# Taking the sixteen gate tiles out of the attention's filling, in a decoder layer on one core

## What is computed

```python
h = rms_norm(x, g_pre_mix)
cb, cc, ch, q, k, v, ga, gb = jnp.split(h @ w_in, IN_SPLITS, axis=-1)
conv_u, conv_state = causal_dwconv(cc * ch, conv_prev, w_conv_a)
y_a = (cb * conv_u) @ w_a
...
z = jnp.einsum('bqhd,bkhd->bhqk', q, k) * (SB_HEAD_DIM ** -0.5) + bias
a = exp(log_beta + later)         # a product of kept shares over later keys
o = jnp.einsum('bhqk,bkhd->bqhd', a, v)
y_b = o @ w_b
merged = jax.nn.sigmoid(ga) * y_a + jax.nn.sigmoid(gb) * y_b
x = x + rms_norm(merged @ w_o, g_post_mix)
```

## Time and profile before

| | before |
|---|---|
| median of 3 runs | 1683.26 us (1683.05 to 1683.74) |
| the profiled execution | 1683.39 us, of which its span is 1681.6 us |
| PE busy, PEld busy | 1668.7 us (99%), 1463.4 us (87%) |
| DVE busy | 1102.6 us (66%) |
| ACT busy | 794.6 us (47%) |
| granted TensorE clock | 1.00 in all slices but the end |

### The profile page before, as it was taken

One profiled execution on the slowest core, in us unless ns is written; L12 is line 12 of the kernel. 1 busy time (PEld: TensorE's weight loads), 2 busy tenths in 40 slices (PEclk: granted clock), 3 DMA queues, 4 the chain that ended last, 5 costly groups with the idle time before them and its releaser, 6 DMA issues. The chain is left out here.

```text
span 1681.6 us, 27183 instructions
## 1 busy us (share of the span) xinstructions
PE 1668.7 (99%) x9107; PEld 1463.4 (87%) x9107; DVE 1102.6 (66%) x1608; ACT 794.6 (47%) x1389; POOL 317.9 (19%) x266
## 2 busy tenths in 40 slices
PE   9999999999999999999999999999999999999998
PEld 8999998999999989988888888888888788888886
DVE  7265246325533647547678888888888698776576
ACT  6445344444534453135444444444444444465675
POOL 1000000000000000003356666666664000000000
PEclk9999999999999999999999999999999999999999
DMA  5312221132123114443132222222222852345333
GB/s 177 102 55 74 78 78 56 57 99 68 61 66 94 51 62 149 155 164 121 62 97 79 79 78 76 73 73 79 79 79 90 300 192 78 94 146 188 108 125 119
DMA packets 176599, 170.66 MB, mean 101 GB/s; under 512 B 16207, under 2 KB 144555, under 8 KB 176492
## 3 DMA queue, kind: packets, MB, share of 16 engines
q1 hardware_dynamic: 165546, 164.41, 30.3%
q10 hardware_dynamic: 10946, 4.91, 1.0%
HBM read 129.66 MB, written 39.62 MB: 101 GB/s over the span
## 5 line engine op out<-in xcount | busy, mean ns | idle before, releaser
L2810 PE MATMUL pair<-xh,wh 128*128 128x384 f32 (+1 forms) x952 | 324.3, 341 | 0.0
L2812 PE MATMUL pair<-xh,wl 128*128 128x384 f32 (+1 forms) x952 | 311.2, 327 | 0.0
L2811 PE MATMUL pair<-xl,wh 128*128 128x384 f32 (+1 forms) x952 | 310.6, 326 | 0.0
L2810 PEld LDWEIGHTS pair<-xh,wh 128*128 128x128 f32 x952 | 179.2, 188 | 5.4 <-issue 4.0
L2811 PEld LDWEIGHTS pair<-xl,wh 128*128 128x128 f32 x952 | 179.3, 188 | 0.0
L2812 PEld LDWEIGHTS pair<-xh,wl 128*128 128x128 f32 x952 | 178.7, 188 | 0.0
L1073 POOL TENSOR_TENSOR srow<-hn,hn 128x512 f32<-128x512 f32 x8 | 12.0, 1506 | 804.1 <-DVE hn L2298 803.8
L3337 PE MATMUL pair<-woph,foph 128*128 128x512 f32 x308 | 120.7, 392 | 0.7 <-DVE fopl L2451 0.7
L3339 PE MATMUL pair<-woph,fopl 128*128 128x512 f32 x308 | 120.0, 390 | 0.0
L3338 PE MATMUL pair<-wopl,foph 128*128 128x512 f32 x308 | 119.9, 389 | 0.0
L1401 ACT ACTIVATE keep<-pair,bias 128x512 f32<-128x512 f32 (+4 forms) x100 | 58.2, 582 | 115.7 <-DVE pair L2151 71.5
(11 more groups left out here) (416 smaller groups left out, 4284.5 us busy)
## 6 DMA issues: line engine op xcount, KB each, us to landing
rawp<-in_w_up SPq DMA_DIRECT2D x88, 256.0 KB, 3.8
raw<-in_w_in SPq DMA_DIRECT2D x80, 256.0 KB, 3.2
wd<-in_w_down SPq DMA_DIRECT2D x55, 256.0 KB, 3.0
f_spill<-cv SPq DMA_DIRECT2D x22, 552.0 KB, 2.8
f<-f_spill SPq DMA_DIRECT2D x44, 256.0 KB, 5.5
gat<-gate_spill SPq DMA_DIRECT2D x16, 544.0 KB, 4.5
x_spill<-x SPq DMA_DIRECT2D x16, 512.0 KB, 3.0
gate_spill<-stg SPq DMA_DIRECT2D x32, 192.0 KB, 1.9
```

The costliest lines, as they stand in the source:

```text
L2810: t_.matmul(b, h, xhi, start=(k == 0), stop=False, skip_group_check=True)
L2811: t_.matmul(b, h, xlo, start=False, stop=False, skip_group_check=True)
L2812: ins = t_.matmul(b, l, xhi, start=False, stop=(k == KD - 1), skip_group_check=True)
```

## The change

The filling keeps three of its seven tiles, the convolution's; the sixteen gate tiles (four for each of the four pairs) are computed after the last pair, in a stage of their own, tile by tile, and the branches follow. The slots stay 28 and the steps in them stay where they are; a slot has two or three pieces in place of six. The sample group's part goes to slots 21 to 24, since the convolution's input is complete only in slot 18. In the new stage PE waits for a bank to be read (`a_gt`), ACT splits the next tile's weights and takes three sigmoids a tile, DVE takes the low part, and SP loads weights two tiles ahead and stores the gates. The split of block 0 of the convolution's output is made by ACT in the stage's last but one tile, and that of block 1 after the stage.

```diff
-STATE_SLOT = 12
-SAMPLE_SLOT = 13
+STATE_SLOT = 21
+SAMPLE_SLOT = 22
 SLOTS = NSTEP + 3
-IN_FILL = 21
-PIECES = IN_FILL * KD // SLOTS
+NIN = 6
+IN_FILL = 9
+GATE_TILES = 2 * KD
+
+def pieces_of(n):
+    return range(IN_FILL * KD * n // SLOTS, IN_FILL * KD * (n + 1) // SLOTS)
...
-FILL_AT = {(KD * i + KD - 1) // PIECES: i for i in range(IN_FILL)}
+FILL_AT = {next(n for n in range(SLOTS) if KD * i + KD - 1 in pieces_of(n)): i for i in range(IN_FILL)}
...
@@ block.sync
+            for t in range(GATE_TILES):
+                load(gate_job(t + 2) if t + 2 < GATE_TILES else ab_job(t + 2 - GATE_TILES))
+                gate_out(t)
...
@@ block.scalar
+            act.wait_ge(d_c, NC4 * NG - NG + 1)
+            for t in range(GATE_TILES):
+                whi()
+                for gr in range(NG):
+                    u = 3 * NIN * NC4 + 3 * t + gr
+                    act.wait_ge(stg_out[gr], stn[gr].at(16 * t))
+                    act.wait_ge(p_unit, punit.at(3 * t + gr + 1))
+                    s_.activation(stg[gr][:, 0:GROUPS[gr][1]], banks[u % 2][:, 0:GROUPS[gr][1]], ACT.Sigmoid).then_inc(a_gt, 1)
+                if t == GATE_TILES - 2:
+                    s_.activation(ch0[:, :], cout[:, 0, :], ACT.Copy).then_inc(a_xhi, 1)
...
@@ block.vector
+            for t in range(GATE_TILES):
+                wlo()
...
@@ block.tensor
-                    for i in range(PIECES):
-                        piece(*divmod(PIECES * n + i, KD))
-                        if n == 0 and i == 2:
+                    for i, p_ in enumerate(pieces_of(n)):
+                        piece(*divmod(p_, KD))
+                        if n == 0 and i == 0:
                             new_rows(vT, 0)
...
+            def gate_tile(t):
+                begin_job()
+                for gr in range(NG):
+                    v_ = 3 * t + gr
+                    if v_ < 2:
+                        pe.wait_ge(d_c, NG * NC4 + v_ - 1)
+                    else:
+                        pe.wait_ge(a_gt, v_ - 1)
+                    b = banks[unit.base % 2][:, 0:GROUPS[gr][1]]
+                    unit.step()
+                    for k in range(KD):
+                        (h, l), xhi, xlo = tall(t % 2, k), part(xh[:, k, :], gr), part(xl[:, k, :], gr)
+                        t_.matmul(b, h, xhi, start=(k == 0), stop=False, skip_group_check=True)
+                        t_.matmul(b, h, xlo, start=False, stop=False, skip_group_check=True)
+                        ins = t_.matmul(b, l, xhi, start=False, stop=(k == KD - 1), skip_group_check=True)
+                    ins.then_inc(p_unit, 1)
+
+            for t in range(GATE_TILES):
+                gate_tile(t)
```

More of the change, by code:

```diff
@@ L744, in pair @@
                     load(in_job(c, n))
[L745 to L755, removed]
-                if not last:
[L757 to L760, removed]
+                    for q in range(2):
+                        values(c, 2 * (n - 4) + q)
+                if not last:
+                    hold(p_m, miscn.at(11))
+                    rows_in(c + 1)
+                    keys(c + 1, 0)
+                    keys(c + 1, 1)
+                for j in range(2):
+                    load(gate_job(j) if last else in_job(c + 1, j))
                 miscn.step(PM_ITER)
-                gtn.step(12)
             hold(g_const, 5)
@@ L767, in _ @@
             keys(0, 1)
-            with loop(sp, NC4 - 1, {job: NIN, miscn: PM_ITER, gtn: 12}) as c:
+            with loop(sp, NC4 - 1, {job: NIN, miscn: PM_ITER}) as c:
                 pair(c, False)
@@ L1338, in natural @@
                     if kind == 0:
+                        if not first:
+                            act.wait_ge(d_c, cn.at(1 - NG))
                         act.wait_ge(stg_out[g], stn[g].at())
@@ L1375, in fill @@
                     b = unit_in(3 + kind, gr)
[L1376 to L1385, removed]
+                    for d, cols in padded(uc, gr):
+                        ins = s_.activation(d, like(b[:, cols], d), ACT.Copy)
+                    ins.then_inc(a_u, 1)
                 for n in range(SLOTS):
@@ L1461, in pair @@
                         soo.step(32)
-                for g in range(NG):
-                    stn[g].step(64)
                 cn.step(NG)
@@ L1487, in _ @@
             for src, dst in ((cout, ch), (oT, oh)):
-                for k in range(2 if src is cout else 0, NC4):
+                for k in range(1 if src is cout else 0, NC4):
                     s_.activation(dst[:, k, :], src[:, k, :], ACT.Copy).then_inc(a_xhi, 1)
@@ L2185, in pair @@
                 for gr in range(NG):
-                    stn[gr].step(80 if gr < 2 else 96)
+                    stn[gr].step(16 if gr < 2 else 32)
             un = Count()
@@ L3048, in pair @@
                             sample_pages()
-                        if n == STATE_SLOT + 2 and i == 2:
+                        if n == STATE_SLOT + 2 and i == 0:
                             sample_turned()
```

55 lines of the change are left out of this document (19 added, 36 removed).

## The result

The changed kernel takes 1732.95 us (median of four runs, 1731.97 to 1734.94) against 1683.49 us before (1683.05 to 1683.74): a ratio of 1.0293, 95% interval 1.0281 to 1.0306, 49.5 us more. The forecast was 1726 us with a range of 1702 to 1754. The profiled execution took 1732.28 us; its span is 1730.6 us, 49.0 more than before.

What follows compares the result with a forecast made beforehand. The prediction took TensorE (PE) to bound the attention. To the profiled 1683.4 us it added 42 us of waits (three pairs at 11, the first at 9) and 0.7 us, giving 1726 us, range 1702 to 1754.

Steps and rivals of the forecast that it cites:

- Moved products: Sixteen gate tiles leave the slots (-189.4 us) and return in their own stage (+189.4), with +0.3 and +0.4 extra.
- the fourth rival: Plain products are faster: gate tiles get the 8% room, slots lose nothing; 15 us less, 1668 us; chance 3%.
- Slot 0: PE waits at the first turning of v for ACT's copy, 2.0 us a pair (1.7 to 2.1).
- Slot 2: First weights ready 3.3 us after the scores, where PE has 2.8 us of work: wait 0.5 us (0 to 1).
- Slot 5: Scores wait for ACT's `beta` of step 4, 1.3 us (0 to 2.5).
- Slots 8 and 10: PE waits for weights behind masks, scan and product: 0.6 and 1.6 us, together 2.2 (1.4 to 3).
- Slots 14 to 18: Same ring with one more DVE operation of 0.2 us a step: waits of 1.1 us (0 to 2).
- Slots 18 to 26: DVE sets the end, with 23.5 us of work against PE's 20.1: wait 3.4 us (1.5 to 5).
- The first pair: Scores with three products instead of two, giving PE 2 us more to cover with: 9 us of waits.
- nothing is lost: Buffers let DVE and ACT run ahead, so PE never waits in the slots: 1684 us; chance 4%.
- The clock falls: Idle PE in the slots drops the clock to 1.2 GHz: about 1943 us; chance 3%.
- The waits feed each other: A late PE makes DVE and ACT late, so every wait in the slots doubles: 1768 us; chance 12%.

Runs made afterwards that it cites:

- e1: Changed kernel with six pieces in slot 0 instead of two, one less in slots 6, 11, 19 and 27; first weight split moves too: 1719.65 us.
- e10: Changed kernel without the 16 masks of the prompt's scores in each pair; ACT's sigmoids wait for the scores instead: 1720.50 us.
- e2: Changed kernel with the weight split of slot 3 issued in slot 6: 1728.91 us.
- e3: Changed kernel with two of three taps of the convolution of c and h left out: 1733.32 us.
- e8: Changed kernel with two of three convolution taps left out and DVE taking up each finished unit one slot later: 1721.52 us.
- e5: Changed kernel with the weight split of slot 21 issued in slot 26: 1728.04 us.
- e9: Changed kernel with DVE taking up each finished unit one slot later, all taps kept: 1728.67 us.
- e4: Changed kernel with the edits of e1, e2 and e3 together: 1714.14 us.
- e6: Changed kernel with a pair's 72 pieces placed where PE waited, six in slot 0 and up to four in later slots: 1724.60 us.
- e11: Changed kernel with e1's table, weight splits in slots 6, 12 and 26, and units taken up one slot later, nothing left out: 1718.97 us.
- e12: e11 with the prompt's masks and two of three convolution taps left out: 1702.41 us.
- e13: Changed kernel with nine useless products added at the start of each of a pair's nine filling units: 1745.93 us.

## Why the prediction was right, and where it was off

The mechanism is the forecast's, and so is the sign. The size was short by 7 us, 49.5 against 42.7: about 2.4 us of it are slots 14 to 18 in three pairs, 1.9 the first pair, and 1.6 the clock behind slot 0 of the fourth. By its own steps:

- *Moved products.* 189.4 us out and in: 189.74 came in; what went out has no row of its own, only its spacing of starts. In the gate stage three products of 384 tokens still take 0.52 us from start to start:

```profile
492.84 0.34 PE L3064 MATMUL pair<-xh,wh 128*128 128x384 f32 x1
...
493.37 0.33 PE L3064 MATMUL pair<-xh,wh 128*128 128x384 f32 x1
```

  So the fourth rival, plain products faster by 15 us, did not come. The rule named beside it, that of the Trainium skill's "Perfetto Trace Analysis", "Identifying the Most-Contended Engine", judges TensorE's room by the share of weight loads and by the FLOP rate. Here the share of weight loads went from 92% in the slots to 100% in the gate stage, and the products' pace is the same in both.
- *Slot 0*, 2.0 us: measured 2.4 in the second pair, 2.2 in the third, of which 0.35 is a wait of its own ahead of the first turning, for ACT's copy of k's rows. The walk had that copy, and took it to be done in time. e1 shows that PE's early arrival makes it: six pieces there, and the wait is gone.
- *Slot 2*, 0.5: 0.5 (from the three turnings at 187.44 to the next start 0.82 us, against 0.33 before), and gone without the masks (e10).
- *Slot 5*, 1.3: 1.3 ahead of the scores and 0.3 ahead of the next turning. The walk had ACT begin once slot 1's masks are in and summed its work up to step 4. The trace agrees at both ends: ACT stands at 186.80 until the masks are in, and `beta` of step 4 ends at 193.72. e2 shows that the weight split of 1.07 us in that sum makes the wait.
- *Slots 8 and 10*, 0.6 and 1.6: measured 0.8 and 1.6 (the last product starts at 200.41 and 205.20, the turning at 201.35 and 206.97), and gone without the masks (e10). The best shown of the terms, since each link of the chain had a row.
- *Slots 14 to 18*, 1.1: measured 1.9. Slot 14 was put at 0.1 and is 0.8. This is the term of the second to fourth pair that was sized worst, by 0.8 us a pair.
- *Slots 18 to 26*, 3.4: measured 3.1. The number held, in part by luck, since its working did not hold as put. It counted all of DVE's work from one product to another, taps among it, as if each microsecond taken off DVE were one off the end. e3 took 3 us of taps off DVE in each pair and nothing off the time, since a unit waits for PE in the midst of that queue; in e8, with the queue's order changed, the same 3 us were worth 7.1 us in four pairs. That DVE sets the end of these slots is shown (it has hardly any idle time there, and e8 nearly ends the waits); that its load does is only half of it.
- *The first pair*, 9: measured 10.9. Its slower scores covered slot 22's wait (0.8) and some of those of slots 0, 2 and 14, while slot 23's is 0.5 longer than in the second pair. It lost 0.9 us less than the third pair, where 2 were allowed.
- *The fourth pair* was taken as like the second and is 1.1 us longer than the third. Its slot 0 has a wait like the others', and behind it the clock at 0.50 for 3.41 us. Of the seven kernels with slot 0's wait as in the changed one (the changed one, e2, e3, e5, e8, e9, e10) six have such a stretch behind it in one pair of the profiled execution, in e3 the third pair; of e1, e4, e6, e11, e12 and e13, in which that wait is gone or short, none has. In how many other executions it falls is not known, nor why it falls in one pair and not in the next.
- Sum: 9.0 and three times 11.0 forecast, 10.9, 12.3, 11.8 and 13.4 measured. *Ends of the stage*, 0.7: 0.6. The 0.06 us for each first weight load (0.7 us a pair) stood on no row, and no run shows it by itself. The two ends of the sum were not made alike: the first pair's 2 us are off the high end (1744) and not off the low one (1702, with them 1700), and the high end leaves out up to 4 us for the ends of the stage.

Of the rivals, *nothing is lost* (1684) is out. *The clock falls* (1943) is out in its size, and the forecast was wrong to let it cost nothing: one stretch of 3.41 us at 0.50 in the profiled execution, about 1.6 us; everywhere else in the slots, the gate stage and the branches the clock is 1.00. *The waits feed each other* (1768) is out in its size, and slot 5 is no case of it, since ACT's lateness from slot 0 ends at 186.80. The 13.3 us of e1 are more than the 9.6 of slot 0's own wait because e1 moved the split too, and had no fall of the clock in its pairs. In the masked and the wide slots a wait that is removed comes back in part at another place (e6, e11); DVE is 26.79 us busy of the 30 from 222 to 252. Its window in the changed kernel:

```profile
222.00:252.00 30.00, 26.93 (x189) 22.02 (x190) 26.79 (x37) 18.21 (x34) 0.00 (x0) 1.00 0.06 19
```

What stays open: how large a filling would lose nothing. At 216 products a pair 11 to 13 us are lost, at 297 about 2, at 504 under 1. A filling of five tiles, 360 products, would be the next kernel to try; it wasn't tried. No version was found that beats the kernel before: it has PE at 99%, and the best one with the change that computes everything, e11, is slower by 2.05% (1.88 to 2.22).

## What to carry to other kernels

When work is taken out from beside a ring of engines, walk the ring place by place with durations of the trace. The load by engine said that PE stays first by 11 us of 76, and 12 us were lost all the same. Ask for each wait how many pieces it is long, what work stands in the chain ahead of it, and whether lateness is handed on or ends at an earlier wait: a row of idle time on the engine in between ends it. Pieces moved to the first wait of the stage won 13.3 us; pieces moved to later waits too cost at other places (e6). And look at what else an edit moves: the table that filled slot 0 moved a weight split as well, which was part of what it won. And an in-order queue that waits for the filling's own result (here DVE for a finished unit) can hide what its other work costs: taking the taps off DVE showed nothing until the order was changed too.

## What the runs showed that I had not expected

Idle PE is nearly free room: 53.8 us of added products cost 13.0 us, though they stood in nine clumps a pair and not where the waits are longest; I had expected the gaps to take 20 us and they took 40.8. And edits did not add: 13.3, 4.0, 4.9 and 4.3 us alone, 14.0 together, while the taps were worth 0 alone and 7.1 us behind another edit. And a wait of under 2 us was followed, in one pair of four, by a stretch at the lower clock.
